# Attention layers of the second block: two projections swapped, three smaller steps moved in the order

## What is computed

```python
for l in range(2):
    h = rmsnorm(x, attn_norm[l])
    sb_q, sb_k, sb_v, df_q, df_k, df_v = split(h @ w_in[l])
    # stick-breaking attention, 8 heads of 64
    z = sb_q @ sb_k.T * scale
    log_keep = where(strict, log_sigmoid(-z), 0)
    between = reverse_cumsum(log_keep) - log_keep
    sb_out = where(strict, exp(log_sigmoid(z) + between), 0) @ sb_v
    # differential attention, 4 heads of 2 x 64, rotary on q and k
    p = softmax(mask(rope(df_q) @ rope(df_k).T * scale))
    df_heads = (p[0] - lam * p[1]) @ df_v
    df_out = rmsnorm(df_heads, subln) * (1 - lambda_init)
    x = x + concat(sb_out, df_out) @ w_o[l]
    x = x + square(relu(rmsnorm(x) @ w_ff1[l])) @ w_ff2[l]
```

## Time and profile before

| what | us |
|---|---|
| runs of the kernel, lowest, median, highest | 2748.66, 2753.75, 2754.22 |
| the profiled execution | 2755.0 |
| its span, first to last instruction | 2753.2 |
| TensorE busy in it | 2706.2 |
| VectorE, ScalarE, GpSimd busy | 1581.5, 1156.2, 628.5 |

### The profile page before, as it was taken

How to read it: one execution, slowest core, us unless ns; L and a number is a source line. 1 busy time by engine, 2 the same in 40 slices (tenths; PEclk the granted TensorE clock), 3 DMA queues, 4 the chain that set the end, 5 groups by cost and what they waited for, 6 DMA issues and landing times.

```text
span 2753.2 us, 31973 instructions
## 1 busy us (share of the span) xinstructions
PE 2706.2 (98%) x12918; PEld 2265.5 (82%) x12918; DVE 1581.5 (57%) x2307; ACT 1156.2 (42%) x1834; POOL 628.5 (23%) x401
## 2 busy tenths in 40 slices
PE   8999999999999999999999999999999999999998
PEld 6888888888878888888888887878888888778886
DVE  6656555344465646565565787644445678734443
ACT  4323322222356636432235777422224767522223
POOL 1000111011136626300005542410113442411100
PEclk9999999999999999999999999999999999999999
DMA  4332323323222222222322211223233221233332
GB/s 153 100 100 92 103 93 100 100 92 100 91 69 64 65 76 65 91 94 98 100 92 94 77 55 46 84 85 98 94 100 102 70 70 32 77 92 94 98 100 69
DMA packets 69412, 238.78 MB, mean 87 GB/s; under 512 B 7696, under 2 KB 10256, under 8 KB 69264
## 3 DMA queue, kind: packets, MB, share of 16 engines
q1 hardware_dynamic: 69264, 236.73, 26.8%
HBM read 234.60 MB, written 2.10 MB: 86 GB/s over the span
## 4 chain that ended last, share of the span: by engine, by line
PE 93%; DVE 4%; POOL 1%; ACT 1%; issue 1%; DMA 0%; SPq 0%; POOLq 0%; DVEq 0%; ACTq 0%
PE ps L414 29%; PE ps L416 29%; PE ps L415 29%; PE ps L510 1%; POOL acc L2280 1%; PE ps L729 1%; PE ps L728 1%; PE ps L440 1%; DVE xl L1518 1%; POOL t L2465 1%; PE ps L714 0%; DVE x L1540 0%; PE ps L571 0%; PE ps L570 0%; DVE ptl L1514 0%
## 5 line engine op out<-in xcount | busy, mean ns | idle before, releaser
L895 ACT ACTIVATE wh<-raw 128x1024 fp32r<-128x1024 f32 (+2 forms) x453 | 465.1, 1028 | 755.9 <-PE ps L416 750.7
L414 PE MATMUL ps<-xh,wh 128*128 128x512 f32 x1920 | 754.2, 393 | 0.0
L416 PE MATMUL ps<-xh,wl 128*128 128x512 f32 x1920 | 747.5, 389 | 0.0
L415 PE MATMUL ps<-xl,wh 128*128 128x512 f32 x1920 | 747.3, 389 | 0.0
L1506 DVE TENSOR_TENSOR wl<-raw,wh 128x1024 fp32r<-128x1024 f32 (+1 forms) x339 | 447.1, 1319 | 155.3 <-ACT wh L895 155.2
L414 PE MATMUL ps<-yh,wh 128*128 128x512 f32 x1088 | 427.7, 393 | 10.6 <-DVE yl L1514 9.0
L415 PE MATMUL ps<-yl,wh 128*128 128x512 f32 x1088 | 424.9, 391 | 0.0
L416 PE MATMUL ps<-yh,wl 128*128 128x512 f32 x1088 | 424.9, 391 | 0.0
L414 PEld LDWEIGHTS ps<-xh,wh 128*128 128x128 f32 x1920 | 360.6, 188 | 77.1 <-issue 2.6
L415 PEld LDWEIGHTS ps<-xl,wh 128*128 128x128 f32 x1920 | 360.6, 188 | 76.5 <-issue 2.6
L416 PEld LDWEIGHTS ps<-xh,wl 128*128 128x128 f32 x1920 | 360.4, 188 | 74.8
(11 more groups left out here) (255 smaller groups left out, 3667.6 us busy)
## 6 DMA issues: line engine op xcount, KB each, us to landing
raw<-in_ff SPq DMA_DIRECT2D x120, 512.0 KB, 3.6
raw<-in_pool_in SPq DMA_DIRECT2D x64, 512.0 KB, 3.3
raw<-in_conv_in SPq DMA_DIRECT2D x64, 512.0 KB, 3.3
raw<-in_pool_out SPq DMA_DIRECT2D x32, 512.0 KB, 3.3
raw<-in_qk SPq DMA_DIRECT2D x32, 512.0 KB, 3.6
raw<-in_pool_grp SPq DMA_DIRECT2D x16, 512.0 KB, 3.3
raw<-in_conv_out SPq DMA_DIRECT2D x16, 512.0 KB, 3.3
raw<-in_mla_z SPq DMA_DIRECT2D x16, 512.0 KB, 3.6
```

The source lines that it names most:

```text
L414: pe.do.matmul(o, lh, rh_, start=start, stop=False)
L415: pe.do.matmul(o, lh, rl_, start=False, stop=False)
L416: return pe.do.matmul(o, ll, rh_, start=False, stop=stop)
L895: act.do.activation(h[:, 0:ncol], r[:, 0:ncol], ACT.Copy).then_inc(*mark("whi", ("whi", k)))
```

## The change

It has four parts, each made in both layers.

- The projections of `dk3` and `sq3` change places, on TensorE, in the order of the weight units, banks and temporaries, and in the sequences of the other engines. TensorE now runs `dk3`, `df_squares(1)`, `sb_pv(3)`, `sq3`, `df_turn(2)`. On ScalarE `turned("dk", 3)` stands ahead of `df_root(1)`, and the weight copy of `taking('sq', l, 3)` behind `keep(4)`. On VectorE `turned("dk", 3)` and `keep(4)` stand ahead of `df_norm(1)` and `project("sq", 3)`. On GpSimd the turn of `dk3` stands ahead of the subtraction of `taking('sq', l, 3)`.
- `sb_scores(7)` stands ahead of `df_squares(3)` on TensorE.
- `df_out(3)` stands ahead of two weight copies on ScalarE.
- The low half of `rot("dq", 3)` stands behind `weights_of(3)` on VectorE.

No instruction is added or removed.

```diff
--- before.py
+++ after.py
@@ -59,11 +59,11 @@
 LAYER_UNITS = (
     ('v', 0, 0, 0), ('v', 0, 0, 1), ('sq', 0), ('sk', 0), ('v', 0, 1, 0), ('dq', 0), ('v', 0, 1, 1), ('dk', 0),
     ('sq', 1), ('dk', 1), ('sk', 1), ('dk', 2), ('dq', 1), ('v', 1, 1, 0), ('v', 1, 1, 1), ('v', 1, 0, 0),
-    ('v', 1, 0, 1), ('dq', 2), ('dq', 3), ('sk', 2), ('sq', 2), ('sq', 3), ('dk', 3), ('sk', 3), ('wo', 0, 0),
+    ('v', 1, 0, 1), ('dq', 2), ('dq', 3), ('sk', 2), ('sq', 2), ('dk', 3), ('sq', 3), ('sk', 3), ('wo', 0, 0),
     ('wo', 0, 1), ('wo', 0, 2), ('wo', 0, 3), ('wo', 1, 0), ('wo', 1, 1), ('wo', 1, 2), ('wo', 1, 3))
 LAYER_BANKS = (
     0, 1, 2, 3, 4, 0, 1, 2, 3, 1, 0, 4, 2, 3, 0, 1, 4, 2, 3, 0, 1, 2, 4, 3, 0, 0, 3, 4, 1, 2, 0, 1, 2, 3, 4, 0, 1,
-    2, 3, 4, 1, 0, 2, 3, 4, 1, 1, 3, 4, 0, 2, 1, 3, 4, 0, 2, 3, 1, 4, 1, 2, 3, 0, 4, 1, 2, 4, 0, 3, 1, 2, 4, 0, 3,
+    2, 3, 4, 1, 0, 2, 3, 4, 1, 1, 3, 4, 0, 2, 1, 3, 0, 4, 2, 3, 1, 4, 1, 2, 3, 0, 4, 1, 2, 4, 0, 3, 1, 2, 4, 0, 3,
     2, 1, 0, 2, 3, 4, 0, 1, 0, 2, 3, 4, 5, 6, 7, 1, 3, 7, 2, 4)
 LAST_BANKS = (0, 5, 6, 1, 3, 7, 2, 4)
 LAST_ROWS = (1, 0, 4, 2, 3, 5, 7, 6)
@@ -270,8 +270,8 @@
                 (("t1", l, "dk", 2), 1), (("t1", l, "dq", 1), 0), (("sw", l, "dq", 2), 2), (("rs", l, 0), 3),
                 (("rt", "df", l, 0), 0), (("sw", l, "dq", 3), 1), (("t1", l, "dq", 2), 0), (("t1", l, "dq", 3), 3),
                 (("pj", l, "sk", 2), 2), (("pj", l, "sq", 2), 1), (("rs", l, 1), 0), (("rt", "df", l, 1), 2),
-                (("sw", l, "dk", 3), 3), (("pj", l, "sq", 3), 1), (("t1", l, "dk", 3), 2), (("pj", l, "sk", 3), 0),
-                (("rs", l, 2), 3), (("rt", "df", l, 2), 2), (("rs", l, 3), 1), (("rt", "df", l, 3), 0),
+                (("sw", l, "dk", 3), 3), (("t1", l, "dk", 3), 1), (("pj", l, "sq", 3), 2), (("pj", l, "sk", 3), 0),
+                (("rs", l, 2), 3), (("rt", "df", l, 2), 1), (("rs", l, 3), 2), (("rt", "df", l, 3), 0),
                 (("sq", 5 + 2 * l, 1), 2), (("sq", 5 + 2 * l, 2), 3), (("sq", 5 + 2 * l, 3), 0),
                 (("sq", 5 + 2 * l, 4), 1), (("sq", 5 + 2 * l, 5), 2), (("sq", 5 + 2 * l, 6), 3),
                 (("sq", 5 + 2 * l, 7), 0)):
@@ -794,13 +794,13 @@
                 sb_between(2), sb_scores(3), df_pv(0), df_scores(1, 32), df_scores(1, 16), proj("dq", 2)
                 df_squares(0), proj("dq", 3), sb_pv(2), proj("sk", 2), proj("sq", 2), df_scores(2, 34)
                 df_turn(1)
-                sb_between(3), df_pv(1), df_scores(2, 32), sb_scores(4), df_scores(2, 16), proj("sq", 3)
-                df_squares(1), proj("dk", 3), sb_pv(3), df_turn(2)
+                sb_between(3), df_pv(1), df_scores(2, 32), sb_scores(4), df_scores(2, 16), proj("dk", 3)
+                df_squares(1), sb_pv(3), proj("sq", 3), df_turn(2)
                 sb_between(4), df_pv(2), df_scores(3, 34), sb_scores(5), df_scores(3, 32), wo(0, 2), wo(0, 0)
                 sb_pv(4), proj("sk", 3), df_scores(3, 16)
                 sb_between(5), wo(0, 1), df_squares(2), sb_scores(6), wo(0, 4), df_turn(3), sb_pv(5), df_pv(3)
                 wo(0, 5), wo(0, 3)
-                sb_between(6), wo(0, 6), df_squares(3), sb_scores(7), sb_pv(6), wo(1, 2, (0, 1))
+                sb_between(6), wo(0, 6), sb_scores(7), df_squares(3), sb_pv(6), wo(1, 2, (0, 1))
                 wo(1, 1, (0, 1)), wo(0, 7), wo(1, 0, (0, 1))
                 sb_between(7), wo(1, 1, (2,)), wo(1, 4, (0, 1, 2)), wo(1, 3, (0, 1, 2)), sb_pv(7)
                 wo(1, 0, (2,)), wo(1, 2, (2,)), wo(1, 1, (3,)), wo(1, 0, (3,)), wo(1, 4, (3,)), wo(1, 2, (3,))
@@ -1371,7 +1371,7 @@
                 taking('sq', l, 2)
                 plain("sk", 2)
                 rot("dq", 3)
-                taking('sq', l, 3)
+                taking('dk', l, 3)
                 plain("sq", 2)
                 df_turn(1)
                 df_exp(2, 34)
@@ -1380,10 +1380,10 @@
                 soft(4)
                 df_exp(2, 32)
                 df_exp(2, 16)
+                turned("dk", 3)
                 df_root(1)
-                taking('dk', l, 3)
-                turned("dk", 3)
                 keep(4)
+                taking('sq', l, 3)
                 df_turn(2)
                 sb_out(3)
                 rot("dk", 3)
@@ -1408,9 +1408,9 @@
                 df_high(2)
                 keep(6)
                 sb_out(5)
+                df_out(3)
                 taking('wo', l, 0, 3)
                 taking('wo', l, 0, 2)
-                df_out(3)
                 weights_of(6)
                 df_root(3)
                 soft(7)
@@ -2113,23 +2113,23 @@
                 project("sk", 2)
                 df_low(0)
                 plain("sk", 2)
-                rot("dq", 3)
                 project("sq", 2)
                 df_max(2, 34)
                 df_turn(1)
                 between(3)
                 plain("sq", 2)
                 weights_of(3)
+                rot("dq", 3)
                 df_max(2, 32)
                 df_max(2, 16)
                 df_eps(1)
                 soft(4)
                 df_sums(2)
                 df_join(2)
-                project("sq", 3)
-                df_norm(1)
                 turned("dk", 3)
                 keep(4)
+                df_norm(1)
+                project("sq", 3)
                 df_turn(2)
                 rot("dk", 3)
                 between(4)
```

## The result

| | median of the runs (lowest to highest) |
|---|---|
| before | 2753.75 us (2748.66 to 2754.99, 5 runs) |
| after | 2740.24 us (2739.74 to 2742.85, 5 runs) |
| after / before | 0.9959, 95% interval 0.9946 to 0.9972 |

The account below looks back on a forecast made before the run. TensorE, busy 98%, bounds the kernel; only its idle and low-clock time can be won. 1.3 + 2.9 + 3.3 = 7.5 us a layer, 15.0 in two, less 1.7 gives 13.3: 2741 us, range 2734 to 2750.

Parts of the forecast that it names:

- The places and the queues: Signs in TensorE's attention layers: three old stalls gone, waits of `sb_pv(6)` (1.4 us) and `df_pv(2)` (0.7 us) instead.
- A1: Transposes of `df_turn(1)` stop after seven for `project("sq", 2)`; moving `rot("dq", 3)` later wins 1.3 us a layer.
- nothing is late next: At `df_turn(1)`: the moved low's readers come later, so the full 1.3 us a layer was taken.
- The ceiling of 1.3: From `df_turn(1)` to `df_pv(1)`: 1.3 us a layer against a TensorE that never waits.
- A2: `sb_between(4)` waits twice for the lows of `keep(4)`; `dk3` ahead of `sq3` wins 2.9 us a layer, bounds 1.5 and 3.6.
- the new idle at `df_pv(2)`: TensorE waits there for VectorE's lows of `df_turn(2)`: 0.7 us, bounds 0 and 2.1.
- the one hold that it counted: GpSimd's subtraction delays VectorE before the lows of `df_turn(2)`: 1.6 us, lows ending about 4.6 us after its start.
- bound of 2.1 us: Upper bound of idle at `df_pv(2)`, if GpSimd holds `keep(4)` too.
- B: `df_squares(3)` waits for `df_eps(3)`; scores ahead and `df_out(3)` early win 3.3 us a layer, bounds 0 and 4.8.
- The counter-case: At `df_eps(3)`: GpSimd stands back for VectorE, as it did from 1619.35, and the place wins 4.8 us instead of 3.3.
- The clock: Falls to 1.2 GHz behind two stalls cost 1.7 and 3.4 us a layer, each counted with its own place.
- one new fall: One fall of the clock somewhere in the two layers, 1.7 us lost, bounds 0 and 2 x 3.4.

Follow-up runs that it names:

- e10: The changed kernel as it is, run again on another chip: median 2741.13 us, 0.9970 of before.
- e8: Changed kernel with `df_out(3)` back behind the two weight copies and the copies of `taking('sq', l, 3)` and `taking('dk', l, 3)` later: 2733.85 us.
- e6: Changed kernel with ScalarE's copy of `taking('sq', l, 3)` moved behind the high parts of `df_turn(2)`: 2740.43 us, 0.9963 of before.
- e4: Kernel before with only `df_out(3)` moved ahead of the two weight copies on ScalarE: 2756.38 us, ratio 1.0024.
- e5: Changed kernel with `df_out(3)` put back behind the two weight copies: 2738.65 us, 0.9960 of before.
- e1: Kernel before with only the low half of `rot("dq", 3)` moved behind `weights_of(3)` on VectorE: 2745.40 us, ratio 0.9978.
- e2: Kernel before with only the swap of `dk3` and `sq3`: 2742.36 us, ratio 0.9968.
- e13: The version with all three copies moved, with `df_squares(3)` put back ahead of `sb_scores(7)`: 2737.12 us, 0.9953 of before.
- e3: Kernel before with only `sb_scores(7)` moved ahead of `df_squares(3)` on TensorE: 2746.53 us, ratio 0.9978.
- e11: The kernel before, unchanged, profiled a second time: 2755.41 us (one run).
- e9: Changed kernel with `df_squares(3)` ahead of `sb_scores(7)` again, `df_out(3)` staying early: 2753.33 us, 1.0009 of before.

## Why the prediction was right, and where it was not

It said 2741 us and 2740.24 came; 13.3 us of gain, 13.5 between the medians. By its own steps the agreement is partly luck: errors on both sides and an accident cancel. The measured 13.5 is itself partly luck, since it hangs on the groups in which the five runs of before fell: on e10's chip the gain was 8.2 us, and the median of all 57 runs of before is 2751.50.

- **The places and the queues: right.** No wait at the eighth transpose, none of `sb_between(4)` on `keep(4)`, `df_squares(3)` with no idle, new waits of `sb_pv(6)` (1.20 us, said 1.4) and `df_pv(2)` (1.09, said 0.7).
- **A1: 0.57 us won, not 1.3.** The step that failed is that nothing is late next. VectorE's last instruction of `df_max(2, 34)`, two columns wide, was held until GpSimd's third subtraction ended, and the lows of `df_turn(1)` stood behind it. In the changed kernel, then in e8, where that subtraction starts later; in each VectorE's instruction and GpSimd's subtractions, of which the third ends at 1629.46 in the changed kernel and starts only at 1630.21 in e8:

```profile
1628.27 1.22 DVE L1691 TENSOR_SCALAR small<-small 128x2 f32<-128x2 f32 x1
...
1621.48 7.98 POOL L2271 TENSOR_TENSOR wl<-raw,wh 128x1024 fp32r<-128x1024 f32 x3
```

```profile
1628.96 0.17 DVE L1691 TENSOR_SCALAR small<-small 128x2 f32<-128x2 f32 x1
...
1622.15 5.66 POOL L2271 TENSOR_TENSOR wl<-raw,wh 128x1024 fp32r<-128x1024 f32 x2
```

  The prediction had looked for holds only among wide instructions with two tile inputs. The ceiling of 1.3 was right: e8 takes 3.86 us for what took 5.19.
- **A2: 2.40 us won, not 2.9, and 0.3 lost at `wo(0, 2)`.** The term that was too small is the new idle at `df_pv(2)`, 0.7 us, measured 1.09. ScalarE's moved copy was costed at 0 us by its reader, `wo`. The prediction did see that the copy releases GpSimd's subtraction, but laid the one hold that it counted on `df_norm(1)`. In fact `df_norm(1)` ran in 0.74 us and the subtraction lay across the third low of `keep(4)` (e6), the case that the prediction had kept for its bound of 2.1 us. The lows ended 5.0 us after the start of `df_turn(2)`, not 4.6. The wait of `wo(0, 2)` was not seen at all.
- **B: right, 3.2 us from `sb_between(6)` to `wo(1, 1)` against 3.3.** `df_eps(3)` took 4.57 us against 4.6 worked out, and the early `df_out(3)` cost 1.2 us against the 1.3 predicted (e4, e5). The Trainium skill ("SBUF — State Buffer", section "Who interferes with whom") has the first to issue keep the port pair; at B and at `keep(4)` the traces agree each time. The counter-case did not come at these places, but it stands in the changed kernel too: GpSimd's sine product took 3.49 us from 1616.57, and four VectorE lows that started behind it, from 1616.69, ran unheld.
- **The clock: wrong in its way of counting.** The prediction gave each place a fall of its own, 1.7 and 3.4 us, and added one new fall. What the runs showed: both falls of a layer are gone when either A1's or A2's stall is (e1, e2), although B keeps its 1.35 us, and that is no luck of two profiles, since each caught one of the slower runs of its kernel; the same 1.35 us cost 4.4 us in before and 1.3 in e13; and no new fall came. So what belongs to the parts does not add up: alone they won 4.2, 5.2, 4.4 and -2.7 us of stretch, 11.1 together, and jointly 5.9 (against before's slowest group, and e4 by its own slowest run).

The sum against the profile: 7.5 us a layer were predicted and 5.9 measured (A1 -0.7, A2 -0.5, `wo(0, 2)` -0.3, B -0.1); the new fall, 1.7 us, did not come; and 3.5 us were won outside the stretches by one execution's better start and a shorter fall. 2 x 5.9 + 3.5 = 15.3.

That the change as a whole is faster is shown by its interval and by e10. That three of its parts win and one costs is shown by e1 to e5. Open is what decides on a fall: 1.9 us of idle (1.27 and 0.67) brought one behind 0.9 us at the transposes (before, e3, e4), and none behind 0.6 at `df_pv(1)` (e1). 1.35 us at B brought one only in the kernel that had one at A2, and 2.5 us at B did in both kernels that had it. One rival was not tested: that the moment at which a stall comes matters beside its length. The groups of before (e11), one kernel at 0.992 and at 0.995, leave room for it.

## What to carry to other kernels

When a step is moved, follow what it releases on every engine, not only who reads its result: a few ScalarE copies with plenty of time decided when GpSimd's subtractions lay across VectorE's path, and moving them was worth half as much again as the change. Price idle time at its own length and the clock's falls for the whole stretch at once, since one small stall fewer can bring back all of them. And where runs lie in groups 3 us apart, judge an edit of 1 us by a stretch between two named instructions, which repeated to 0.1 us, not by the median. That holds only between profiles with the same falls of the clock, so look at these and at each run's granted clock first.

## What the runs showed of the hardware

- A VectorE `TENSOR_SCALAR` of two columns, one input, took 1.22 us under a GpSimd subtraction instead of 0.17. The Trainium skill ("SBUF — State Buffer", section "Who interferes with whom") counts `tensor_scalar` among the operations that can take the shared port pair; this trace agrees.
- The same stall of 1.35 us was followed by 6.8 us at 1.2 GHz (before), and by none (e1, e2, e13); 2.5 us by 10.2 us at 1.2 GHz (the profiled executions of e4 and e9, both among the slower of their kernels). A fall of 6.8 us cost 3.1 us: 17.1 against 14.0 from `sb_between(6)` to `wo(1, 1)` with the same wait.
- Fewer falls can come with more idle time: 4.7 us of idle and none (e1), 4.2 us and two (before).
- The same kernel had a mean granted clock of 0.995 in its ten fastest runs and 0.992 in its slowest, 9 us apart (before, 57 runs).
